# Low-rank stage and recurrence joined in one block, with the first tile's chain beside the last low-rank products

## What is computed

```python
w_lo = jnp.tanh(x_w @ w_in[:, c[4]:c[5]])
a_lo = x_a @ w_in[:, c[5]:c[6]]
w_raw = (w0 + w_lo @ w_up).astype(f32)
log_decay = -jnp.exp(-jax.nn.softplus(-w_raw) - 0.5)
a = jax.nn.sigmoid((a0 + a_lo @ a_up).astype(f32))
kk = heads(k * k_k)
kk = kk / jnp.maximum(jnp.sqrt(jnp.sum(kk * kk, axis=-1, keepdims=True)), 1e-12)
k = k.astype(f32) * (1.0 + (a - 1.0) * k_a.astype(f32))
# for every token, with the state S of each head:
sa = jnp.einsum('bhvk,bhk->bhv', S, -kk_t)
S = S * w_t[:, :, None, :] + sa[..., None] * (kk_t * a_t)[:, :, None, :] + v_t[..., None] * k_t[:, :, None, :]
y_t = jnp.einsum('bhvk,bhk->bhv', S, r_t)
# second layer, bias of the windows:
bias = rel_bias[buckets].astype(jnp.float32).transpose(2, 0, 1)
```

## Time and profile before

| | us |
|---|---|
| median of 3 runs (3200.6 to 3204.63) | 3203.28 |
| the profiled execution's own time | 3206.4 |
| its span | 3204.5 |
| PE busy in the span | 2900.4 (91%) |
| DVE, ACT, POOL busy | 1602.9, 1081.4, 604.4 |

### The profile page before, as it was taken

One profiled execution on the slowest core, in us unless ns is written; L12 is line 12 of the kernel. 1 busy time (PEld: TensorE's weight loads), 2 busy tenths in 40 slices (PEclk: granted clock), 3 DMA queues, 4 the chain that ended last, 5 costly groups with the idle time before them and its releaser, 6 DMA issues. The chain is left out here.

```text
span 3204.5 us, 78691 instructions
## 1 busy us (share of the span) xinstructions
PE 2900.4 (91%) x35058; PEld 2396.7 (75%) x35058; DVE 1602.9 (50%) x2633; ACT 1081.4 (34%) x2002; POOL 604.4 (19%) x412
## 2 busy tenths in 40 slices
PE   7999999997668888887886999999999997999699
PEld 4887888886357777877785778888777896777487
DVE  5433333433076677776763663222477204777662
ACT  3223332322535454453552441010222103546310
POOL 5522222110022232322321220000000001034230
PEclk8999999998879999999998999999999998999899
DMA  5123321211733432323305761111111216223672
GB/s 168 60 89 112 112 89 63 79 50 39 249 104 89 114 111 82 100 69 95 102 24 151 232 183 33 33 40 40 40 60 66 89 45 210 80 70 109 215 249 85
DMA packets 342032, 322.79 MB, mean 101 GB/s; under 512 B 14095, under 2 KB 257167, under 8 KB 341056
## 3 DMA queue, kind: packets, MB, share of 16 engines
q1 hardware_dynamic: 313104, 258.31, 26.5%
q10 hardware_dynamic: 24480, 47.21, 4.1%
q0 software_dynamic: 4112, 12.25, 1.2%
HBM read 199.77 MB, written 122.64 MB: 101 GB/s over the span
## 5 line engine op out<-in xcount | busy, mean ns | idle before, releaser
L327 PE MATMUL pj_ps<-pj_x_hi,pj_w_hi 128*128 128x512 f32 x1024 | 402.3, 393 | 9.1 <-DVE pj_w_lo L260 4.6
L327 PE MATMUL pj_ps<-pj_x_lo,pj_w_hi 128*128 128x512 f32 x1024 | 400.4, 391 | 0.0
L327 PE MATMUL pj_ps<-pj_x_hi,pj_w_lo 128*128 128x512 f32 x1024 | 400.1, 391 | 0.0
L1761 PE MATMUL dm_ps<-h_hi,dm_w_hi 128*128 128x512 f32 x896 | 279.6, 393 | 0.0
L1761 PE MATMUL dm_ps<-h_lo,dm_w_hi 128*128 128x512 f32 x896 | 275.8, 389 | 0.0
L1761 PE MATMUL dm_ps<-h_hi,dm_w_lo 128*128 128x512 f32 x896 | 275.8, 389 | 0.0
L200 POOL TENSOR_TENSOR pj_x<-h 128x512 f32<-128x512 f32 x128 | 166.4, 1301 | 485.4 <-DVE pj_x_lo L255 435.8
L255 DVE TENSOR_TENSOR pj_x_lo<-pj_x,pj_x_hi 128x512 fp32r<-128x512 f32 x128 | 92.3, 721 | 318.6 <-ACT pj_x_hi L347 318.5
L327 PEld LDWEIGHTS pj_ps<-pj_x_hi,pj_w_hi 128*128 128x128 f32 x1024 | 193.4, 189 | 53.1 <-DVE pj_w_lo L260 7.1
L327 PEld LDWEIGHTS pj_ps<-pj_x_lo,pj_w_hi 128*128 128x128 f32 x1024 | 193.3, 189 | 40.7 <-issue 0.7
L327 PEld LDWEIGHTS pj_ps<-pj_x_hi,pj_w_lo 128*128 128x128 f32 x1024 | 193.4, 189 | 40.6
(11 more groups left out here) (256 smaller groups left out, 5923.7 us busy)
## 6 DMA issues: line engine op xcount, KB each, us to landing
proj<-pj_out ACTq DMA_DIRECT2D x128, 256.0 KB, 2.4
pj_w<-w_in SPq DMA_DIRECT2D x32, 512.0 KB, 4.1
proj<-lr_out SPq DMA_DIRECT2D x32, 512.0 KB, 4.5
dm_w<-w_out SPq DMA_DIRECT2D x32, 512.0 KB, 5.0
dm_w<-w_in SPq DMA_DIRECT2D x32, 512.0 KB, 4.8
partial<-wa_ob SPq DMA_DIRECT2D x48, 264.0 KB, 2.1
mo_part<-partial SPq DMA_DIRECT2D x16, 792.0 KB, 9.3
wa_vt<-v_rows SPq DMA_DIRECT2D x43, 260.0 KB, 3.0
```

The costliest lines, as they stand in the source:

```text
L327: mm = pe.matmul(ps[i][:], wp, xp, start=k == 0 and m == 0, stop=k == KT - 1 and m == len(parts) - 1)
L1761: last = pe.matmul(PS[:, 2 * i + b, :], wp, hp[:, k, t0:t0 + 512], start=k == 0 and m == 0, stop=k == KT - 1 and m == len(parts) - 1)
```

## The change

1. The two functions become programs inside one block. The low-rank buffers are taken ahead (`low_rank_buffers`), each engine runs its low-rank list and then its recurrence list, and the barrier between them is gone. Where a buffer of the recurrence lies over one of the low-rank stage, explicit waits stand: SP waits for all `lr_h_low` subtractions and the first eight stores before its first loads, PE for all sigmoids before the spread of tile 0, ACT for all stores before `rw_b_tok`. The allocation order of the recurrence changes to fit.
2. SP issues the nine first loads (kkr, cst, sw, basic, two of spread_g, a, k, r) after the store of n = 15, ahead of the stores of n = 16 to 31. The load of `v` stays in the step.
3. ACT squares kkr of tile 0 between `low(3)` and `sigmoids(2)`; PE sums it by head between `raised(2)` and `raised(3)`; the table load for logarithm and exponential comes after the last sigmoid.
4. On DVE, in the step of tile 0 alone, all four decay sums and the two `rw_am` come ahead of the clamp.
5. The three DMAs from `lines` to `skew` leave the recurrence, and POOL issues them one after the other in `dense_middle`, after the last product of the output projection.

```diff
-def rwkv_low_rank(nc, h, vec, w_in, w_up, a_up, proj, rel_bias, onehot, lines):
+def low_rank_programs(sems, buffers, h, vec, w_in, w_up, a_up, proj, rel_bias, onehot, lines):
...
+    def sync(sp, ahead):
...
+        for n in range(NB * KT):
+            b, j = n // KT, n % KT
+            sp.wait_ge(s_sig, 2 * n + 2)
+            sp.dma_start(proj_rows[4:6, :, j, cols(b)].rearrange("q p t -> p q t"),
+                         out[n % 4][:]).then_inc(s_out[n % 4], 16)
+            if n == 2 * KT - 1:
+                sp.wait_ge(s_h_lo, NB * KT)
+                for i in range(4):
+                    sp.wait_ge(s_out[i], 16 * (KT // 4))
+                ahead()
...
+    def tensor(pe, between):
...
+        for b in range(1, NB):
+            down(b)
+            raised(b - 1)
+        pe.wait_ge(s_lo, 2 * NB)
+        between()
+        raised(NB - 1)
+
+    def scalar(act, between):
...
+        for b in range(1, NB):
+            if b + 1 < NB:
+                high(b + 1)
+            low(b)
+            if b == NB - 1:
+                between()
+            sigmoids(b - 1)
+        sigmoids(NB - 1)
...
-            load(0, "kkr", 6, [])
-            sp.dma_start(cst[:], consts).then_inc(s_const, 16)
-            load(0, "sw", 4, [])
...
+            def first_loads():
+                load(0, "kkr", 6, [])
+                sp.dma_start(cst[:], consts).then_inc(s_const, 16)
+                load(0, "sw", 4, [])
...
+            low_sync(sp, first_loads)
             run(sp, step)
...
         @block.gpsimd
         def _(pool):
+            low_gpsimd(pool)
             pool.wait_ge(s_const, 64)
...
             def step(n, f, b):
-                if b and b.t % 2 and b.t < 2 * len(DILATIONS):
-                    heads = slice(b.t // 2 * HEADS, (b.t // 2 + 1) * HEADS)
-                    pool.dma_start(skew[heads].rearrange("n (p x) -> n p x", x=SKEW),
-                                   lines[heads].unsqueeze(1).to_broadcast([HEADS, 128, SKEW])).then_inc(s_skew, 16)
...
+                if f and f.t == 0:
+                    for i in range(4):
+                        act.wait_ge(s_low_out[i], 16 * (T // 512 * KT // 4))
                 if f:
                     tokens_of(f, 0, b_tok)
...
-            key_squares(0)
+            low_scalar(act, lambda: key_squares(0))
+            act.preload_act_table_set("natural_log_exp_and_others")
+            act.wait_ge(s_const, 64)
+            act.wait_ge(s_init, INITS)
             run(act, step)
...
             def step(n, f, b):
+                if n and not f:
+                    for i in range(4):
+                        decay_sums(n, i)
+                    key_gains(n, f)
                 if n:
                     n.need("ksum")
...
-            key_sums(0)
+            def first_sums():
+                pe.wait_ge(s_const, 64)
+                key_sums(0)
+
+            low_tensor(pe, first_sums)
+            pe.wait_ge(s_low_sig, 2 * (T // 512) * KT)
+            pe.wait_ge(s_init, INITS)
             run(pe, step)
...
             pool.memset(zu[:, T + 1:T + 2], 0.0).then_inc(s_zero, 1)
+            for g in range(len(DILATIONS)):
+                heads = slice(g * HEADS, (g + 1) * HEADS)
+                pool.dma_start(skew[heads].rearrange("n (p x) -> n p x", x=SKEW),
+                               lines[heads].unsqueeze(1).to_broadcast([HEADS, 128, SKEW])).then_inc(s_skew, 16)
```

More of the change, by code:

```diff
@@ new lines, in low_rank_buffers, with sb @@
+def low_rank_buffers(nc, c):
+    def sb(n, shape, dt=F32):
+        return c.enter_context(nc.sbuf_tensor(f"lr_{n}", shape, dt))
+    lo_w, here, back = (sb(n, [128, KT, 2 * RANK]) for n in ("lo_w", "here", "back"))
+    w_hi, w_lo = ([sb(f"{n}{i}", [128, KT, 2 * RANK], F32R) for i in range(2)] for n in ("w_hi", "w_low"))
+    h_hi, h_lo = ([sb(f"{n}{i}", [128, KT, 513], F32R) for i in range(2)] for n in ("h_hi", "h_low"))
+    up = sb("up", [128, D])
+    lo = sb("lo", [128, T])
+    out = [sb(f"out{i}", [128, 2, 512]) for i in range(4)]
+    rb = sb("rb", [BUCKETS + 1, HEADS])
+    hot = sb("hot", [BUCKETS + 1, len(DILATIONS), SKEW])
+    flat = sb("flat", [HEADS, len(DILATIONS), SKEW])
+    up_ps = [c.enter_context(nc.psum_tensor(f"lr_up{i}", [128, 2, 512], F32)) for i in range(3)]
+    down_ps = [c.enter_context(nc.psum_tensor(f"lr_down{i}", [128, 512], F32)) for i in range(2)]
+    return (lo_w, here, back, w_hi, w_lo, h_hi, h_lo, up, lo, out, rb, hot, flat, up_ps, down_ps)
@@ L682, in rwkv_recurrence @@
         dec = [sb(f"dec{i}", [128, KT, NCH]) for i in range(2)]
-        sq, am, bt, kt, rk, bv = (sb(n, tile) for n in ("sq", "am", "bt", "kt", "rk", "bv"))
+        sq, am, bt, rk = (sb(n, tile) for n in ("sq", "am", "bt", "rk"))
+        v_in = [sb(f"v{i}", tile) for i in range(2)]
+        kt, bv = sb("kt", tile), sb("bv", tile)
         yv = [sb(f"yv{i}", tile) for i in range(2)]
@@ L1021, in m_next, with key_gains @@
                                         dec[f.t % 2][:, :, ci:ci + 1].to_broadcast([128, KT, RW_N]), ALU.mult), "m_sb")
+            def key_gains(n, f):
+                n.need("in_a")
+                if f:
+                    f.need("rk")
+                n.did(dve.scalar_tensor_tensor(am[:], a_in[:], -1.0, bc("k_a"), ALU.add, ALU.mult), "am")
+                n.need("am")
+                n.need("in_k")
+                n.did(dve.scalar_tensor_tensor(am[:], am[:], 1.0, k_in[:], ALU.add, ALU.mult), "kp")
             def step(n, f, b):
+                if n and not f:
+                    for i in range(4):
+                        decay_sums(n, i)
+                    key_gains(n, f)
                 if n:
```

313 lines of the change are left out of this document (135 added, 178 removed).

## The result

The changed kernel takes **3183.62 us** (median of 7 runs, 3164.59 to 3189.03). The kernel before, run beside it on the same chip, takes 3205.75 (7 runs, 3200.6 to 3214.36). The ratio is 0.9921, with a 95% interval from 0.9897 to 0.9945, so some 25 us are gone. Two later pairs on other occasions gave 0.9898 (0.9872 to 0.9925) and 0.9924 (0.9907 to 0.9940). The prediction was 3172.5, a gain of 30.8, with a range of 3160 to 3185.

A forecast was written before the change was run, and what follows sets the result against it. PE is busy for 91% of the span, so gains lie where it idles. Border 20.2 plus skew DMAs 10.6 is 30.8: profiled 3206.4 becomes 3175.6, with the median 3.1 below, 3172.5 us; range 3160 to 3185.

The forecast's parts named there:

- E + 12.1: First big product of tile 0 starts 12.1 us after E, the end of the last sigmoid.
- How much later E comes: Loads ahead of n = 16's store delay E, the end of the last sigmoid, by 5.0 us.
- the two bounds: Last sigmoid's end: 3 us earlier if ACT alone sets the pace, 15 later if all stores go at low rate.
- loads hidden: Border rival: the last sigmoid's end doesn't move, gain 25.2 + 10.6, total 3167.5 us; chance 0.13.
- PE's clock in the border: When ACT and PE stand still, the lr_up matmuls would then start at 1.2 GHz; 0 to 2 us.
- Border gain 20.2: Between last sigmoid and recurrence, tile 0's first product comes at 881.5 instead of 901.73 us: gain 20.2.
- Skew DMAs: Moving the three DMAs out of the recurrence's 13 steps saves 10.6 us.
- the 17: Upper bound in us for the recurrence's gain, measuring its three skew steps against the shortest step shown.
- skew gives nothing: Recurrence rival: the stalls are PE's own hunger for code and appear elsewhere; 3183.1 us; chance 0.15.
- New place of the skew DMAs: Start of the convolution: their issue costs 0, at most 5 us, with 5.9 us of cover for h_lo.
- the rival of a slower fetch in the joined block: Recurrence: PE's instruction fetch falls back in 16 steps, 3.5 us each, 56 against 30.8; 3228 us; chance 0.03.
- the three signs by which the prediction falls: Last sigmoid ends beyond 875, recurrence steps' mean rises above 50, or PE idles at the convolution's start.

The follow-up runs named there:

- the one in which k comes late: Changed kernel with kkr and constants issued behind n = 7's store, and k and r behind n = 27's store; 3174.00 us, ratio 0.9914.
- the early loads: Changed kernel with kkr and constants (1.75 MB) issued behind n = 7's store, once the last h_lo is done; 3167.44 us, ratio 0.9897.
- the skew part alone: Kernel before with only the three skew DMAs moved to dense_middle; 3188.66 us against 3202.72, ratio 0.9957.

## Why the prediction was right, and where it was not

**What bounds the kernel: right.** All that was gained is PE's idle time at the two places named.

**E + 12.1: right to 0.1 us.** It is 11.9 to 12.1 in every joined kernel but the one in which k comes late (12.5). Table load, logarithm, exponentials, spread and kk come in the order and with the lengths taken from the earlier trace rows. kk, where I kept a price of 1.2, starts 0.3 us after POOL's `rw_bt` and takes 1.22, so 8.1 was the right one of the two. `rw_ar` behind it takes 1.95 instead of the 3.36 of the earlier trace rows, since it starts 1.3 later and waits for the same end of POOL's instruction. By the Trainium skill ("SBUF — State Buffer", section "Who interferes with whom") kk, with one SBUF input, goes through beside GpSimd, and the trace agrees: 1.22 us beside POOL's 2.41.

**How much later E comes: right mechanism, too small.** Two terms were mis-sized. I counted 18.1 us for the loads, 2.5 behind two stores and 15.6 from the earlier trace rows, and let n = 16's store follow at 1.45. They took from 835.25 to some 854.6 (r's issue at 846.10 and its 8.5 us), 19.4 in all, and the store came 1.3 behind them. And I took 0.6 off, from 5.6 to 5.0, for a jam served without a gap. That did not come: from the landing of n = 16's store to E it is 17.2 us, and before it was 17.0 (its store landed 4.7 after 842.71). So E moved by 7.1 us in the means (29.7 against 22.6), not 5.0. The experiments give the reason in part. Two more loads cost 2.3 us per 512 KB, where my 15.6 for 3.9 MB comes to 2.1. The prediction also called the 4.5 us of the earlier trace rows that of a lone store; it is the median of all 32, most of them in a full queue. The square was counted as free; once the loads are early it is on the path, and taking it away gives 1.3. Whether it costs anything in the changed kernel itself, where SP was busy issuing loads until 847.91, was not tried. Of the two bounds the true value lay near my choice. The rival "loads hidden" was wrong for this kernel, and it is what the early loads bring about: 22.2 us, as before the change.

**PE's clock in the border: right.** The first `lr_up` products behind the 6.96 us of standing still run at the 1.2 GHz level (granted clock 0.50, then 0.86), and ACT waits 1.33 us for PE there. The low clock came as foreseen, but a price of it inside E isn't shown: ACT waited 1.29 us for PE in this run of sigmoids before the change too, with the clock at 1.00 (the row below), and E comes 17.2 us behind the landing of n = 16's store instead of 17.0. With the early loads PE doesn't stop and the clock is 1.00 there. ACT before, then windows of the changed kernel, then of the early loads:

```profile
847.44 1.27 ACT L565 ACTIVATE lr_out<-lr_up,vec 128x512 f32<-128x512 f32 x2 [1.29 <-PE lr_up L536]
```

```profile
855.00:860.00 5.00, 2.73 (x12) 1.14 (x14) 1.18 (x1) 3.91 (x7) 0.00 (x0) 0.50 0.76 263
860.00:865.00 5.00, 5.00 (x30) 2.26 (x26) 0.28 (x1) 3.67 (x7) 0.00 (x0) 0.86 1.02 314
```

```profile
855.00:860.00 5.00, 4.28 (x18) 1.11 (x16) 0.00 (x0) 4.63 (x9) 0.00 (x0) 1.00 1.03 392
```

**Border gain 20.2: measured 18.4,** the 2.1 of E short and little else.

**Skew DMAs: right cause, 10.6 was too small.** The part alone brought 14 us in the timed runs, and the three steps went from 158.6 to 144.9 in the means, 14. What was mis-sized is the "three usual ones" of 49.7 that I compared with. The ten others of the first trace were long by chance (497.4 in all, 489.7 in the second, 486.5 to 495.5 in all the later ones). And the second, fourth and sixth step are shorter than the others even without skew DMAs: 48.3 each, where the other ten take 49.1 in the nine traces without them. Of the two bounds the 17, against the shortest step, was the nearer one. The rival "skew gives nothing" is out: the steps are short in the changed kernel and in the skew part alone, long with the DMAs put back, and longer with them twice.

**New place of the skew DMAs: right.** From the memset of `dm_zu` to DVE's taking of the first result it is 20.0 us before and after (1896.35 to 1916.37 now), and the stretch to the end is not longer in the skew part alone. The cover of 5.9 us was not even needed: DVE starts its scaling 3.6 us after the memset in both kernels, and PE is busy for 23.00 of the 23 us around this start in both, with a DMA share of 0.97 where it was 0.19.

**The sum.** The gain expected was 30.8 and the two places gave 33.3 in the means, but only some 26 arrived. What I had no term for is the loss of 7 us in stages that the change does not touch: 1.6 behind the first product, 3.1 in the last steps, 1.5 in the output projection, 1.2 at the end. The first is PE's clock. The granted clock from the first product to the start of the 13 steps is 0.75, 0.75 and 0.66 in the three traces of the changed kernel and 0.85 in both of before; the skew part, with the old block, has 0.66 and 20.6 us as well, so it is not the joined block. That the total lies in the range at all is thus in part luck: the skew DMAs gave 3 to 4 us more than forecast, the border 2 less, and 7 were lost elsewhere. The part in the output projection is of the size by which two executions of one kernel differ there. The 3.1 of the last steps is in all traces of after; where it comes from is open, and two other joined kernels have only 140.5 and 140.9 there, so it may be chance. No trace supports the rival of a slower fetch in the joined block: its steps are those of the old one, with and without skew DMAs. None of the three signs by which the prediction falls is there: the last sigmoid ends at 873.03, the 13 steps average 49.1 us, and PE doesn't idle at the start of the convolution.

## What to carry to other kernels

A stretch in which the DMA engines stand still is the place for loads; put ahead of a store that an engine waits for, a load costs its full time at the load's rate (2.3 us for 512 KB here), and even one issued behind such a store costs some. In this kernel a long DMA beside a stretch of many small instructions of PE (1408 matmuls in some 49 us) took its price in idle time for issue, and beside large matmuls (101 in 23 us) it took none. When a term is a difference of steps, compare the same steps without the cause, or take a second trace of the kernel before: two traces of it differed by 7.6 us in 13 steps.

## What the runs showed of the hardware

- **The price of DMAs beside small matmuls grows faster than the bytes, but not in issue stalls.** 4.5 MB of skew DMAs cost 14 us in three steps, the next 4.5 MB in the same steps 20. PE's idle time for issue rose by 13.5 us with the first set (42.8 to 56.3 in the means) and by 12 at most with the second (54.6 to 66.5).
- **SP's issue becomes slow when many loads are queued.** `basic`, 128 KB, took 3.99 us to issue as the fourth of nine behind the stores, 1.16 as the fourth of nine in the kernel before, where no store was left ahead of it, and 0.43 as the third in the kernel with early loads, where the DMA engines had just stood still.
- **The clock falls behind some short waits and not behind others.** A wait of PE of 3.26 us in the output projection was followed by 5 us at 0.56 and 5 at 0.75; one of 2.53 at the same place in another execution of the same kernel left it at 1.00. After a longer fall its return differs too: the mean over the 20 us from the first product is 0.66 to 0.76 in eight of the thirteen traces, where this stretch takes 20.0 to 21.1 us, and 0.85 to 0.90 in the other five, where it takes 19.1.
- **A later load slows an earlier store of the same queue.** Two sigmoid pairs waited 0.61 and 1.27 us for stores issued ahead of k and r. The Trainium skill ("DMA: Bandwidth & Descriptors", section "Queues, rings and completion order") says that descriptors are taken in ring order but that a later one may finish its write before an earlier one. No run here shows a later one finish first: the store ahead of k landed at 868.1 and k at 869.6. What the trace shows is that the earlier store took 5.7 us instead of 3.9.
